# Probabilities times values, head by head, in a one-core attention layer in split float32

## What is computed

```
h    = rms_norm(x, norm_pre_g)
proj = h @ w_in                      # q k v g of FoX, 8 forget columns, q k v g of MoBA
y_a  = softmax(q k^T / 8 + F[t] - F[s], causal) @ v * silu(g),  F = cumsum(log_sigmoid(f + b))
y_b  = softmax(q k^T / 8 - slope * (t - s), causal) @ v * silu(g)
out  = x + rms_norm(concat(y_a, y_b) @ w_out, norm_post_g)
```

## Time and profile before

| | |
|---|---|
| median of 3 runs | 150.39 us (149.98 to 150.87) |
| the profiled execution: its own time | 150.02 us |
| its span | 148.2 us |
| granted TensorE clock, mean | 0.997 of full speed |
| busy: PE / DVE / ACT / POOL | 138.7 / 108.3 / 94.1 / 52.6 us |

### The profile page before, as it was taken

How to read it: one execution, slowest core, us unless ns; L and a number is a source line. 1 busy time by engine, 2 the same in 40 slices (tenths; PEclk the granted TensorE clock), 3 DMA queues, 4 the chain that set the end, 5 groups by cost and what they waited for, 6 DMA issues and landing times.

```text
span 148.2 us, 2971 instructions
## 1 busy us (share of the span) xinstructions
PE 138.7 (94%) x1060; PEld 129.4 (87%) x1060; DVE 108.3 (73%) x234; ACT 94.1 (64%) x193; POOL 52.6 (36%) x74
## 2 busy tenths in 40 slices
PE   7679999999999999999999999999999999999930
PEld 7558999999999999999999999999999888898830
DVE  0359837899999999879898888687879774222591
ACT  5279588668967578797576686676838373234340
POOL 2069200000000061039194857557290936020411
PEclk9999999999999999999999999999999999999998
DMA  4899999399865999953544444434290000000034
GB/s 85 252 338 336 350 404 342 85 352 268 286 191 202 383 398 332 316 209 87 197 146 142 142 142 148 139 109 143 66 383 15 2 0 0 0 4 0 0 142 142
DMA packets 9725, 26.96 MB, mean 182 GB/s; under 512 B 1384, under 2 KB 2416, under 8 KB 9456
## 3 DMA queue, kind: packets, MB, share of 16 engines
q1 hardware_dynamic: 9120, 25.57, 50.6%
q10 hardware_dynamic: 592, 1.22, 2.2%
HBM read 25.73 MB, written 1.06 MB: 181 GB/s over the span
## 4 chain that ended last, share of the span: by engine, by line
PE 86%; DMA 5%; issue 3%; POOL 2%; DVE 1%; ACT 1%; POOLq 1%; DVEq 0%; ACTq 0%
PE bank L830 46%; PE bank L840 14%; PE bank L987 11%; PE bank L941 6%; PE bank L924 5%; DMA wf<-in_w_f 4%; DMA gpre_col<-in_g_pre 2%; PE bank L932 1%; PE bank L933 1%; PE bank L931 1%; POOL x_t L361 1%; POOL h L358 1%; POOLq L72 1%; ACT squares L539 0%; PE bank L887 0%
## 5 line engine op out<-in xcount | busy, mean ns | idle before, releaser
L563 DVE TENSOR_TENSOR w_lo<-raw,w_hi 128x1024 fp32r<-128x1024 f32 (+1 forms) x33 | 43.9, 1335 | 4.6 <-ACT w_hi L375 4.3
L375 ACT ACTIVATE w_hi<-raw 128x1024 fp32r<-128x1024 f32 (+1 forms) x33 | 34.5, 1057 | 6.3 <-PE bank L830 2.6
L830 PE MATMUL bank<-h_hi,w_hi 128*128 128x256 f32 x128 | 36.4, 285 | 0.0
L830 PE MATMUL bank<-h_lo,w_hi 128*128 128x256 f32 x128 | 35.7, 279 | 0.0
L830 PE MATMUL bank<-h_hi,w_lo 128*128 128x256 f32 x128 | 35.7, 279 | 0.0
L309 POOL TENSOR_TENSOR bias<-squares,causal 128x256 f32<-128x256 f32 (+1 forms) x8 | 12.9, 1627 | 37.5 <-DMA squares<-decay_rows_scratch 37.5
L830 PEld LDWEIGHTS bank<-h_hi,w_hi 128*128 128x128 f32 x128 | 24.1, 188 | 1.2
L830 PEld LDWEIGHTS bank<-h_lo,w_hi 128*128 128x128 f32 x128 | 24.0, 188 | 0.2
L326 POOL TENSOR_TENSOR probs<-probs,row_inv 128x256 f32<-128x256 f32 (+1 forms) x16 | 12.9, 827 | 31.7 <-DVE row_inv L705 31.7
L830 PEld LDWEIGHTS bank<-h_hi,w_lo 128*128 128x128 f32 x128 | 24.1, 188 | 0.0
L830 PE MATMUL bank<-xg_hi,w_hi 128*128 128x256 f32 x64 | 17.8, 278 | 0.0
(11 more groups left out here) (121 smaller groups left out, 304.9 us busy)
## 6 DMA issues: line engine op xcount, KB each, us to landing
raw<-in_w_units SPq DMA_DIRECT2D x30, 512.0 KB, 4.8
raw_out<-in_w_out SPq DMA_DIRECT2D x4, 512.0 KB, 6.0
raw<-in_w_out SPq DMA_DIRECT2D x4, 512.0 KB, 3.5
h<-in_x SPq DMA_DIRECT2D x2, 512.0 KB, 7.9
squares<-decay_rows_scratch ACTq DMA_DIRECT2D x1, 1024.0 KB, 6.0
x_t<-in_x SPq DMA_DIRECT2D x1, 1024.0 KB, 6.5
raw<-in_w_units SPq DMA_DIRECT2D x3, 256.0 KB, 5.3
out<-x_t SPq DMA_DIRECT2D x3, 256.0 KB, 2.0
```

The costliest lines, as they stand in the source:

```text
L375: nc.scalar.activation(w[0][:, s, 0:width], raw[:, s, 0:width], ACT.Copy).then_inc(s_hi, 1)
L563: nc.vector.tensor_tensor(w[1][:, s, 0:width], raw[:, s, 0:width], w[0][:, s, 0:width].bitcast(F32), ALU.subtract).then_inc(s_lo, 1)
L830: last = nc.tensor.matmul(dst, stationary(a, j), moving(b, j), start=n == 1, stop=n == count * len(PASSES))
```

## The change

There are three parts.

1. **`values` goes head by head.** The tile v now holds, for each head, its 64 high columns and its 64 low columns side by side. For each head the stationary operand is these 128 columns and the moving operand the high part of that head's own probabilities; the low part of the probabilities meets only the 64 high columns. Rows 0 to 63 of pv_ps then hold high x high plus high x low, rows 64 to 127 the low x high part of the same head. ACT copies rows 64 to 127 of each head out of PSUM (`cross_rows`, into y_cross), DVE adds the rows 0 to 63 to them (into y_sum), then multiplies with the gate in one instruction of 128 rows. `cross_rows(i-2)` is the last step of a pair in ACT's program. PE may overwrite pv_ps when the sums are made.
2. **The last steps of PE are in another order.** Pairs 4 and 5 of the groups 2, 3 and 4 are multiplied before the wait for the last pair's y, and after it all five groups have only pairs 6 and 7 left.
3. **wf is loaded before ACT waits for the norm's gain**, not after the first xg_hi.

```diff
@@ -87 +87 @@
-        v = sb("v", [P, 2 * TT, D_MODEL], F32R)
+        v = sb("v", [P, TT, 2 * HEADS, 2, HEAD_DIM], F32R)
@@ -98,0 +99,2 @@
+        y_cross = sb("y_cross", [P, SEQ])
+        y_sum = sb("y_sum", [P, SEQ])
@@ -179,0 +182 @@
+        s_ycross, s_ysum = sem("y_cross_ready"), sem("y_sum_ready")
@@ -384,0 +388 @@
+            act.dma_start(wf[:, :, :], w_f).then_inc(s_wf_in, 16)
@@ -399,2 +402,0 @@
-                if c == 0:
-                    act.dma_start(wf[:, :, :], w_f).then_inc(s_wf_in, 16)
@@ -428,2 +430,3 @@
-                nc.scalar.activation(v[:, t, lo:hi], v_banks[t][c][:, 0:hi - lo], ACT.Copy,
-                                     scale=rstd[:, t:t + 1]).then_inc(s_vhi, 1)
+                nc.scalar.activation(v[:, t, lo // HEAD_DIM:hi // HEAD_DIM, 0, :],
+                                     v_banks[t][c][:, 0:hi - lo].rearrange("p (n d) -> p n d", d=HEAD_DIM),
+                                     ACT.Copy, scale=rstd[:, t:t + 1]).then_inc(s_vhi, 1)
@@ -476 +479 @@
-                act.wait_ge(s_y, 2 * i + 2)
+                act.wait_ge(s_y, i + 1)
@@ -478,0 +482,6 @@
+            def cross_rows(i):
+                act.wait_ge(s_pv, i + 1)
+                for a, own in enumerate(head_rows):
+                    nc.scalar.activation(y_cross[own, :], pv_ps[head_rows[1], a, :], ACT.Copy).then_inc(s_ycross, 1)
@@ -514,0 +524,2 @@
+                if first == 0:
+                    cross_rows(i - 2)
@@ -530,0 +542 @@
+            cross_rows(PAIRS - 2)
@@ -532,0 +545 @@
+            cross_rows(PAIRS - 1)
@@ -620,2 +633,4 @@
-                nc.vector.scalar_tensor_tensor(out=v[:, TT + t, lo:hi], in0=v_banks[t][c][:, 0:hi - lo],
-                                               scalar=rstd[:, t:t + 1], in1=v[:, t, lo:hi].bitcast(F32),
+                heads = slice(lo // HEAD_DIM, hi // HEAD_DIM)
+                nc.vector.scalar_tensor_tensor(out=v[:, t, heads, 1, :],
+                                               in0=v_banks[t][c][:, 0:hi - lo].rearrange("p (n d) -> p n d", d=HEAD_DIM),
+                                               scalar=rstd[:, t:t + 1], in1=v[:, t, heads, 0, :].bitcast(F32),
@@ -717,6 +732,10 @@
-            def gated(i):
-                dve.wait_ge(s_pv, i + 1)
-                for a in range(2):
-                    rows = slice(a * HEAD_DIM, (a + 1) * HEAD_DIM)
-                    nc.vector.tensor_tensor(y32[rows, :].unsqueeze(1), pv_ps[rows, a:a + 1, :],
-                                            gate[rows, bass.ds(i, 1), :], ALU.mult).then_inc(s_y, 1)
+            def gated(i, freed=None):
+                dve.wait_ge(s_ycross, 2 * i + 2)
+                for a, own in enumerate(head_rows):
+                    nc.vector.tensor_tensor(y_sum[own, :], pv_ps[head_rows[0], a, :], y_cross[own, :],
+                                            ALU.add).then_inc(s_ysum, 1)
+                if freed is not None:
+                    dve.wait_ge(s_ylo, freed)
+                dve.wait_ge(s_ysum, 2 * i + 2)
+                nc.vector.tensor_tensor(y32[:, :].unsqueeze(1), y_sum[:, :].unsqueeze(1),
+                                        gate[:, bass.ds(i, 1), :], ALU.mult).then_inc(s_y, 1)
@@ -747,3 +766 @@
-                    if not (isinstance(i, int) and i == 2):
-                        dve.wait_ge(s_ylo, i - 2)
-                    gated(i - 2)
+                    gated(i - 2, None if isinstance(i, int) and i == 2 else i - 2)
@@ -765,2 +782 @@
-            dve.wait_ge(s_ylo, PAIRS - 2)
-            gated(PAIRS - 2)
+            gated(PAIRS - 2, PAIRS - 2)
@@ -768,2 +784 @@
-            dve.wait_ge(s_ylo, PAIRS - 1)
-            gated(PAIRS - 1)
+            gated(PAIRS - 1, PAIRS - 1)
@@ -938,5 +953,9 @@
-                order = [(0, PASSES[0])] + [(1, x) for x in PASSES] + [(0, x) for x in PASSES[1:]]
-                for n, (t, (x, z)) in enumerate(order):
-                    dst = pv_ps if t == 0 else pv_ps[:, :, P:SEQ]
-                    last = nc.tensor.matmul(dst, v[:, x * TT + t, i * P:(i + 1) * P], (p_t0, p_t1)[t][z][:, :, :],
-                                            start=n == 0, stop=n == len(order) - 1)
+                for a in range(2):
+                    both, high = pv_ps[:, a, :], pv_ps[head_rows[0], a, :]
+                    v_0, v_1 = (v[:, t, 2 * i + a, :, :] for t in range(TT))
+                    nc.tensor.matmul(both, v_0, p_t0[0][:, a, :], start=a == 0, stop=False)
+                    if a == 0:
+                        nc.tensor.matmul(both[:, P:SEQ], v_1, p_t1[0][:, a, :], start=False, stop=False)
+                    nc.tensor.matmul(high[:, P:SEQ], v_1[:, 0, :], p_t1[1][:, a, :], start=False, stop=False)
+                    nc.tensor.matmul(high, v_0[:, 0, :], p_t0[1][:, a, :], start=False, stop=False)
+                last = nc.tensor.matmul(both[:, P:SEQ], v_1, p_t1[0][:, a, :], start=False, stop=True)
@@ -973 +992 @@
-                    pe.wait_ge(s_y, 2 * i - 4)
+                    pe.wait_ge(s_ysum, 2 * i - 4)
@@ -1003 +1022 @@
-            pe.wait_ge(s_y, 2 * PAIRS - 4)
+            pe.wait_ge(s_ysum, 2 * PAIRS - 4)
@@ -1009 +1028 @@
-            pe.wait_ge(s_y, 2 * PAIRS - 2)
+            pe.wait_ge(s_ysum, 2 * PAIRS - 2)
@@ -1012,2 +1031,3 @@
-            out_part(3, range(0, 4))
-            out_part(4, range(0, 4))
+            out_part(3, range(0, 6))
+            out_part(4, range(0, 6))
+            out_part(2, range(4, 6))
@@ -1016,2 +1036,2 @@
-            for g, first in enumerate((6, 6, 4, 4, 4)):
-                out_part(g, range(first, PAIRS)).then_inc(s_group, 1)
+            for g in range(len(out_groups)):
+                out_part(g, range(6, PAIRS)).then_inc(s_group, 1)
```

## The result

| | before | after |
|---|---|---|
| median of 20 runs each | 150.0 us | 152.39 us |
| ratio of the runs, 95% interval | | 1.0132 [1.0101, 1.0163] |
| profiled execution: its time, its span | 150.02, 148.2 us | 151.11, 149.3 us |
| busy PE / DVE / ACT / POOL | 138.7 / 108.3 / 94.1 / 52.6 us | 137.9 / 114.2 / 100.5 / 53.0 us |

The forecast was no change (150.0, range 148.1 to 151.8). The change costs 2.0 us by the ratio, 2.4 by the medians. Single traces differ by their start: those of kernels with the changed start enter the loop between 66.3 and 68.0 us, so traces are compared by stretches inside them.

A forecast was written before the change was run, and what follows sets the result against it. PE, with 86% of the chain that ended last, was taken as the bound; -1.3 - 0.35 + 1.4 = -0.25 us from 150.02 gave 149.8, set at 150.0 towards the median of 150.39, range 148.1 to 151.8.

The forecast's parts named there:

- three signs of being wrong: PE waits inside the loop, 128-column matmuls start under 0.1 us apart, or the second norm factor comes within 2.3 us.
- Values step, 0.89 us per pair: PE's values matmuls in each pair: 0.89 us instead of 1.05, saving 1.3 us in eight pairs.
- the absence of a drain: PE's values step: no cost for changing stationary columns; the rival with draining said net +6.5 us, 156.5, chance 0.11.
- short matmuls are cheap: Rival on PE's values step: 128-column matmuls with a short weight load cost half, net -1.5 us, 148.5, chance 0.18.
- Extra work of ACT and DVE at nothing: In the loop, ACT's copies and DVE's added instruction cost nothing, covered by 1.4 us of DVE's idle time.
- The statement that y has no reader until the projection: In the loop, POOL's y_low and the high part of y were said to have no reader before the projection.
- The rival of the bound loop: Later sums exceed the 1.4 us cover: 0.25 us in each of six pairs, net +1.25, 151.2, chance 0.09.
- wf, 0.35 us: Earlier load of wf at the start: saves 0.35 us, with 0 to 0.9 as ends.
- the cap: PE's fourth gate unit waits for the bank DVE's gate product frees, so only 0.37 us of lead survives.
- The end, 1.4 us: After PE's last matmul, DVE's list starts at T - 0.43, second norm factor at T + 3.2: end 1.4 us later.
- The sum: All terms together against the profiled execution of 150.02 us: -0.25 us, giving 149.8 us.

The follow-up runs named there:

- no_cross: The changed kernel without ACT's copies of the cross rows and DVE's sums, the low values' part of y left out: 148.52 us, ratio 0.993.
- bias_wait: The changed kernel with POOL's second bias piece waiting for DVE's low part of the weights, and POOL's loops written out: 149.30 us, ratio 0.9996.
- tail_only: The kernel before with the new order of the output projection alone: 151.72 us, ratio 1.0142.

## Why the prediction was wrong, step by step

Two of its three signs of being wrong came: PE waits inside the loop, and 128-column matmuls start 0.06 us apart.

- **Values step, 0.89 us per pair.** The price of 256 columns and the absence of a drain were right, the price of 128 columns was not: 0.06 and not 0.11 (its rival "short matmuls are cheap"). The step takes 0.71 plus 0.06 behind it; worth 2.5 us, not 1.3. The row of the two 128-column matmuls that "cost 0.105 each" was the change to and from 8 columns with a late operand, and equal durations say nothing on the distance between starts: the durations of 128 and 256 columns in the values step are 222 and 280 ns, but one costs half the other. The Trainium skill (TensorE: Matmul & The Clock Gate, Back-to-back issue gap) gave 56 ns; this trace agrees with 0.06.
- **Extra work of ACT and DVE at nothing.** This is the step that failed. The prediction took 1.4 us of idle time on DVE as cover for it. It read this in the one pair of six in which w_lo takes 1.23 us; the next pair has 0.91, and no_cross, with the shorter values step, 1.18. And the price left out the wait for ACT's copies (0.39), that for DVE's own sums (0.22), the stretch of the product (0.56 for 0.425), and above all that a w_lo started later falls behind POOL's bias: 1.97 us, 2.30 in the FoX pairs. The statement that y has no reader until the projection was wrong too: y_high stands ahead of q_hi on ACT. The rival of the bound loop had the mechanism, but 0.25 us per pair; it cost 0.4 to 0.75 in all but the first of seven, 3.0 us together. bias_wait gives back 2.0 of them by keeping w_lo from standing behind the bias.
- **wf, 0.35 us.** 0.6 [0.2, 1.0] by its own run, in the range given. The reason for the cap was wrong: DVE's gate product came 1.19 us earlier too (36.89 for 38.08), with the w_lo in front of it (35.74 for 36.94). What released DVE's queue earlier was not traced.
- **The end, 1.4 us.** The mechanism held to 0.05 us (T - 0.48 for T - 0.43), the list then took 4.10 us where the forecast had 3.67: two sums of ms took 0.90 us beside POOL's x_t (142.22 to 143.81) and 0.46 before the change, the residual 0.13 less, and the 0.12 us taken off for a wait were not saved. The end costs 1.85 us by the traces (T + 7.85 for T + 6.0) and 2.1 by tail_only.
- **The sum.** -1.3 - 0.35 + 1.4 was -0.25. Measured: -2.5 (values) + 3.0 (loop) - 0.6 (wf) + 2.1 (end) = +2.0 us, which is what the ratio says. The errors on values, wf and end (-1.2, -0.25, +0.7) came to -0.8; the 3.0 us counted at zero decided.

## What to carry to other kernels

Before extra work is hidden under an idle time, take the idle time from the loop as it will be, in every kind of pair, and ask of each instruction that will start later what it will start behind. Where a low-part subtraction with both operands in SBUF meets POOL, the order of starts is worth more than the work: a wait on POOL made this kernel 2 us faster. When PE gets faster by 0.3 us per pair, the other engines have 0.3 us less.

## What the hardware showed that was not expected

Two instructions that each read two operands from SBUF, one of DVE and one of POOL, do not share: the later stands until the earlier has ended, and is shown busy all the while. k_lo, with one operand in PSUM, keeps its 0.42 us beside POOL's norms (98.80 in the changed kernel). 0.89 + 1.08 = 1.97, 1.23 + 1.07 = 2.30 (a FoX pair) and 0.53 + 1.08 = 1.61 us for w_lo on DVE, which alone takes 1.22 (1.08 us of it come behind the other's end); 1.12 + 0.61 = 1.73 for y_low on POOL, which alone takes 0.75. The Trainium skill (SBUF — State Buffer, SBUF: two separate sides) calls it an exclusive lock held for the whole instruction by whichever starts first; this case's runs agree, and in bias_wait w_lo falls to 1.23 us once the bias waits for it. In float32r a matmul of 128 columns in the values step starts 0.06 us before the next, also between stationary tiles of 128 and 64 columns (weight loads of 188 and 135 ns). The rule of the Trainium skill that changing the tiling mode drains TensorE (TensorEngine Tiling (Array Packing), Key Properties) does not show here for columns.
